# Stick-breaking attention stage rewritten as one unrolled pipeline over four pairs of heads

## The reference

```python
def sb_attend(q, k, v, q_pos0):
    z = jnp.einsum('bqhd,bkhd->bhqk', q, k).astype(jnp.float32) * SCALE
    vis = jnp.arange(nk)[None, :] < (q_pos0 + jnp.arange(nq))[:, None]
    log_fail = jnp.where(vis, jax.nn.log_sigmoid(-z), 0.0)
    log_w = z + lax.cumsum(log_fail, axis=3, reverse=True)
    w = jnp.exp(jnp.where(vis, log_w, NEG))
    out = jnp.einsum('bhqk,bkhd->bqhd', w.astype(v.dtype), v)
```

## Time and profile before

| | us |
|---|---|
| median of 3 runs (1680.41 to 1681.86) | 1681.58 |
| span of the profiled execution, which is also its own time | 1681.6 |
| from the first product of the stage for branch B to its last weighted sum | 409.6 |

### The profile page before, as it was taken

How to read it: one execution, slowest core, us unless ns; L and a number is a source line. 1 busy time by engine, 2 the same in 40 slices (tenths; PEclk the granted TensorE clock), 3 DMA queues, 4 the chain that set the end, 5 groups by cost and what they waited for, 6 DMA issues and landing times.

```text
span 1681.6 us, 27158 instructions
## 1 busy us (share of the span) xinstructions
PE 1590.9 (95%) x9750; PEld 1456.5 (87%) x9750; DVE 767.6 (46%) x1319; ACT 558.3 (33%) x1167; POOL 476.3 (28%) x404
## 2 busy tenths in 40 slices
PE   6998999989898898898999999999999999999996
PEld 5987998878797887897888898998989989899894
DVE  6363473765847668745543313223132231322318
ACT  6354364444443344533333121211212112121123
POOL 2101111342423424242004232322323223232234
PEclk9999999999999999999999999999999999999998
DMA  6111212121021211345222111201112012021123
GB/s 182 49 52 47 61 43 61 44 70 51 25 72 42 57 51 50 122 146 184 105 79 67 50 54 34 62 25 50 57 30 62 27 48 62 26 62 32 43 101 143
DMA packets 129922, 110.44 MB, mean 66 GB/s; under 512 B 14472, under 2 KB 118192, under 8 KB 129872
## 3 DMA queue, kind: packets, MB, share of 16 engines
q1 hardware_dynamic: 122960, 101.11, 19.6%
q10 hardware_dynamic: 6912, 8.65, 1.4%
HBM read 87.94 MB, written 21.80 MB: 65 GB/s over the span
## 4 chain that ended last, share of the span: by engine, by line
PE 77%; issue 9%; DVE 8%; ACT 3%; POOL 1%; DMA 1%; SPq 0%; ACTq 0%; POOLq 0%; DVEq 0%
PE m_ya L1493 20%; PE m_yb L1493 10%; PE m_yb L1515 9%; PE b_gm L893 8%; PE a_gm L443 6%; PE a_gm L479 4%; PE m_ya L1515 4%; DVE b_fail L1073 3%; PE b_gm L915 3%; PE m_ya L1546 3%; PE m_yb L1546 2%; PE b_tb L990 2%; DVE b_wgt L1076 1%; PE a_ob L544 1%; ACT b_wgt L873 1%
## 5 line engine op out<-in xcount | busy, mean ns | idle before, releaser
L1312 POOL TENSOR_TENSOR w_lo<-f_raw,w_hi 128x1024 fp32r<-128x1024 f32 x66 | 157.9, 2399 | 406.5 <-ACT w_hi L1363 406.5
L1493 PE MATMUL m_ya<-x_hi,w_hi 128*128 128x352 f32 x704 | 227.3, 323 | 1.2 <-DVE x_lo L1628 0.9
L1493 PE MATMUL m_ya<-x_lo,w_hi 128*128 128x352 f32 x704 | 225.6, 320 | 0.0
L1493 PE MATMUL m_ya<-x_hi,w_lo 128*128 128x352 f32 x704 | 225.6, 320 | 0.0
L1363 ACT ACTIVATE w_hi<-f_raw 128x1024 fp32r<-128x1024 f32 x66 | 68.2, 1050 | 213.3 <-PE m_yb L1483 209.3
L1493 PEld LDWEIGHTS m_ya<-x_hi,w_hi 128*128 128x128 f32 x704 | 132.0, 188 | 2.5 <-issue 1.0
L1493 PEld LDWEIGHTS m_ya<-x_hi,w_lo 128*128 128x128 f32 x704 | 132.3, 188 | 0.4
L1493 PEld LDWEIGHTS m_ya<-x_lo,w_hi 128*128 128x128 f32 x704 | 132.0, 187 | 0.0
L1681 DVE TENSOR_TENSOR f_yacc<-m_yb,f_yacc 128x512 f32<-128x512 f32 x132 | 90.9, 690 | 82.0 <-PE m_yb L1515 81.6
L1493 PE MATMUL m_yb<-x_hi,w_hi 128*128 128x352 f32 x352 | 113.6, 323 | 0.0
L1493 PE MATMUL m_yb<-x_hi,w_lo 128*128 128x352 f32 x352 | 113.0, 321 | 0.0
(11 more groups left out here) (245 smaller groups left out, 3961.2 us busy)
## 6 DMA issues: line engine op xcount, KB each, us to landing
f_raw<-in_w_gate_up_dram SPq DMA_DIRECT2D x44, 512.0 KB, 3.9
w_raw<-in_w_in_dram SPq DMA_DIRECT2D x33, 512.0 KB, 4.0
f_raw<-in_w_down_dram SPq DMA_DIRECT2D x22, 512.0 KB, 3.4
m_gate<-gate_scratch SPq DMA_DIRECT2D x16, 528.0 KB, 4.3
gate_scratch<-a_gst ACTq DMA_DIRECT2D x24, 176.0 KB, 1.9
gate_scratch<-b_gst ACTq DMA_DIRECT2D x24, 176.0 KB, 1.9
xtok<-in_x_prompt_dram SPq DMA_DIRECT2D x8, 512.0 KB, 3.4
w_raw<-in_w_out_dram SPq DMA_DIRECT2D x8, 512.0 KB, 4.1
```

Source lines behind the costliest of these rows:

```text
L1312: pool.tensor_tensor(w_lo[:, j % 3, :, :].rearrange("p k n -> p (k n)"), raw[:, j % 2, :], w_hi[:, j % 3, :, :].rearrange("p k n -> p (k n ...
L1493: last = pe.matmul(gm[c][:, 0:CW], w[:, j % 3, k, :], x[:, k, chunk(c)], start=(k == 0 and n == 0), stop=(k == KT - 1 and n == 2))
```

## The change

The stage for branch B is no longer a loop: it is written out for all pairs. `ORDER` and `TURN` number all transposes of the stage in one sequence.

- Only q, k and v of the first pair are computed ahead (9 chunks). All other tiles, in the order q, k, v of the next pair and one gate tile, are strewn over the nine steps of the pair before: 288 products in each of the pairs 0 to 2, 348 in pair 3 (five gate tiles), 12 behind it. `STEP` holds the products of each step, and `fills` cuts them into those between the second head's scores, ahead of the transposes, between second groups, and behind the weighted sums.
- `b_qs`, `b_kh`, `b_kl` and `b_vtok` have two buffers, in turn by pair.
- TensorE does transposes and weighted sums of the step before with no products in between, and the rest of the step's products behind the sums. k's and v's tokens of the next pair are turned in steps 6 and 7, the cache's keys in step 5.
- ScalarE: between the first and the second head's sigmoids come the chunks that the first products end (`chunk_out`, with k's and v's copies, which VectorE did) and in step 5 the cache's high parts; behind the output the others. At each tile's second chunk it splits the tile after next.
- GpSimd: both heads' selects, then the low parts of the tiles that are due (`los`).
- VectorE: the first head's scan and multiply, then the cache's low parts, the copies of the turned weights, the tokens, the low parts of chunks (`chunk_out`), then the second head's scan and multiply.
- Outputs of both branches are stored to DRAM (`o_dram`), branch A's by ScalarE's queue at the end of each of its two turns, branch B's in thirds by SP, and loaded for the merge in three chunks. The splits of the first two chunks and of the merge's first weight tile are done within the stage. SP waits for all gate stores ahead of the last chunk.

```diff
@@ branch A, ScalarE
+                    act.wait_ge(o_out, past(g * NSTEP + NSTEP))
+                    act.dma_start(o_dram[bass.ds(g * 2, 2), :, :].rearrange("o p t -> p o t"),
+                                  ot[:, bass.ds(g * 6, 2), :]).then_inc(o_stored, 16)
@@ branch B, the plan
-            FILL = [(0, 3, 0, 3)] * 4 + [(3, 4, 0, 4)] + [(5, 2, 4, 4)] * 3 + [(0, 12, 4, 4), (0, 5, 0, 5)]
+            STEP = [[6, 19, 26, 33, 40, 46, 54, 60, 4]] * (NP - 1) + [[8, 24, 33, 42, 50, 58, 66, 55, 12]]
+            LAST = 12
+
+            def fills(s):
+
+                if s == NS:
+                    return 0, 0, 0, LAST
+                f, i = STEP[s // NT][s % NT], s % NT
+                z, g = f // 8, f // 10 if s and GROUPS[(s - 1) % NT] > 1 else 0
+                rest = f - z * PIECES[i] - 2 * g
+                return z, rest // 2, g, rest - rest // 2
@@ SP, behind the last pair
+                for n in range(2):
+                    sp.wait_ge(gate_stored[n], 16 * KT * NCH // 2)
...
+                for done in (b_out, *b_stored):
+                    sp.wait_ge(*done)
+                load_o(sp, 2)
@@ GpSimd
+                for s in range(NS):
+                    q = ROWS[s % NT]
+                    for a in range(2):
+                        hs = 2 * s + a
+                        pool.wait_ge(z_read, piece(s, a, PIECES[s % NT] - 1) + 1)
+                        for buf, slot, fill in ((fail, hs % NF, 1.0), (wgt, hs % NW, 0.0)):
+                            diag = buf[0:q, slot, SEQ - q:SEQ]
+                            pool.affine_select(out=diag, in_=diag, compare_op=ALU.is_gt, fill=fill, base=0,
+                                               pattern=[[-1, q]], channel_multiplier=1).then_inc(masked, 1)
+                    if s:
+                        los([*chunks(s - 1, False), *chunks(s - 1, True)])
@@ ScalarE
+                    elif kind == 1:
+                        act.activation(kvt[:, chunk(c)], gm[c][:, 0:CW], ACT.Copy).then_inc(vt_ready, 1)
                         for a in range(2):
                             for half in range(2):
+                                last = act.activation(kh[n % 2][half * HD:(half + 1) * HD, a, chunk(c)],
                                                       gm[c][a * HD:(a + 1) * HD, 0:CW], ACT.Copy)
                         last.then_inc(stack_hi, 1)
...
+                    if c == 1 and 3 <= T + 2 < NTILE:
+                        hi(T + 2)
...
+                for s in range(NS + 1):
+                    pair, i = divmod(s, NT)
+                    if s < NS:
+                        for a in range(2):
+                            if a:
+                                for r in chunks(s, False):
+                                    chunk_out(r)
+                                if i == 5:
+                                    for b in range(2):
+                                        act.wait_ge(turned, TURN["c", pair, b] + 1)
+                                        act.activation(kch[:, b, :], tb[TURN["c", pair, b] % 2][:, 0:PAST], ACT.Copy).then_inc(kc_hi, 1)
+                            hs, q, n = 2 * s + a, ROWS[i], KEYS[i]
+                            need(act, w_ready, hs - NF + 1)
...
+                    if s:
+                        out(s - 1)
+                    for r in chunks(s, True):
+                        chunk_out(r)
@@ TensorE
+                        for a in range(2):
+                            for j in range(PIECES[i]):
+                                if a:
+                                    products(at, nz)
+                                    at += nz
+                                z = zb[piece(s, a, j) % 2][0:q, :]
+                                need(pe, z_read, piece(s, a, j) - 1)
...
+                    products(at, na)
+                    at += na
...
+                                t = TURN["w", s - 1, g, a]
+                                if g:
+                                    products(at, ng)
+                                    at += ng
...
+                            pe.wait_ge(turned_out, TURN["w", s - 1, g, 1] + 1)
...
+                    products(at, nc_)
+                    at += nc_
@@ VectorE
+                for s in range(NS + 1):
+                    pair, i = divmod(s, NT)
+                    if s < NS:
+                        weights(s, 0)
+                    if s < NS and i == 5:
+                        for a in range(2):
+                            dve.wait_ge(kc_hi, pair * 2 + a + 1)
...
+                                last = dve.tensor_copy(wt[:, g, a, 0:len(full), 0:q], src[:, 0:len(full), 0:q])
...
+                    if i in (6, 7) and pair < NP - 1:
+                        tok_out("kv"[i - 6], pair + 1)
+                    for r in chunks(s, False):
+                        chunk_out(r)
+                    if s < NS:
+                        weights(s, 1)
+                    for r in chunks(s, True):
+                        chunk_out(r)
```

More of the change, by code:

```diff
@@ L103, in bank, with need @@
         return ctx.enter_context(nc.psum_tensor(name, [P, 512], F32))
+    def need(engine, semaphore, count):
+        if count > 0:
+            engine.wait_ge(semaphore, count)
     with ExitStack() as outer:
@@ L721, in build @@
[L721 to L729 removed]
+            THIRDS = [slice(0, 3 * P), slice(3 * P, 6 * P), slice(6 * P, TOKENS)]
+            BLOCKS = [range(4), range(4, 8), range(8, 9)]
+            W = w_in[0].rearrange("(k p) n -> p k n", p=P)
@@ new lines, in build, with filled @@
+            LAST = 12
[6 more added lines that the diff above has]
+                return z, rest // 2, g, rest - rest // 2
+            def filled(s, end):
+                before = sum(sum(fills(e)[1:]) + fills(e)[2] + fills(e)[0] * PIECES[e % NT] for e in range(s))
+                z, a, g, c = fills(s)
+                return before + (z * PIECES[s % NT] if s < NS else 0) + a + (2 * g + c if end else 0)
@@ L731, in blocks_of, with piece @@
+            TURN = {key: n for n, key in enumerate(ORDER)}
+            def piece(s, a, j):
+                pair, i = divmod(s, NT)
+                return pair * NZ + 2 * sum(PIECES[:i]) + a * PIECES[i] + j
             def blocks_of(i):
@@ new lines, in los @@
+                def los(done):
+                    for r in done:
+                        if r % NCH == 1 and 3 <= r // NCH + 2 < NTILE:
+                            lo(r // NCH + 2)
+                        if r == NCH * (NTILE - 1):
+                            pool.wait_ge(m_first_hi, 1)
+                            pool.tensor_tensor(w_lo[:, 0, :, :], m_raw[0], w_hi[:, 0, :, :].bitcast(F32),
+                                               ALU.subtract).then_inc(m_first_lo, 1)
+                lo(1)
@@ L885, in _ @@
             @block.tensor
             def _(pe):
-                for mine in (gemm_done, turned, z_done, o_done):
-                    pe.sem_inc(mine, CREDIT)
-                def gemm(p, j, c):
-                    for k in range(KT):
-                        for n, (w, x) in enumerate(((w_hi, x_hi), (w_lo, x_hi), (w_hi, x_lo))):
-                            last = pe.matmul(gm[c][:, 0:CW], w[:, SLOT[j], k, :], x[:, k, chunk(c)],
-                                             start=(k == 0 and n == 0), stop=(k == KT - 1 and n == 2))
-                    last.then_inc(gemm_done, 1)
@@ L918, in gates, with tokens @@
                             last.then_inc(gemm_done, 1)
+                def tokens(kind, pair):
+                    for n, blocks in enumerate(BLOCKS):
+                        t = TURN[kind, pair, n]
+                        src = kvt if kind == "k" else vvt
+                        pe.wait_ge(vt_ready, 6 * pair + (3 if kind == "v" else 0) + min(n + 2, NCH))
+                        need(pe, turned_out, t - 1)
+                        for m, i in enumerate(blocks):
+                            last = pe.transpose(tb[t % 2][0:ROWS[i], m * P:(m + 1) * P], src[:, toks(i)], ident[:, :])
+                        last.then_inc(turned, 1)
                 pe.wait_ge(*a_units_split)
```

675 lines of the change are left out of this document (347 added, 328 removed).

## The result

The changed kernel takes 1714.3 us (median of 4 runs, 1710.9 to 1718.2) against 1681.7 (4 runs, 1680.4 to 1683.0): 1.0193 times the time of before, 95% interval 1.0174 to 1.0211, 32.5 us slower. The forecast was 1687, slower, with 1651 to 1704 as its range; the time lies outside.

The account below looks back on a forecast made before the run. TensorE is busy for 95% of the span, so only its waits or slow running can be won. 1681.6 + 0.7 (between branches) + 8.3 (stage) - 3.8 (merge) = 1686.8, say 1687 us, range 1651 to 1704.

Parts of the forecast that it names:

- the term for the clock: Branch B's stage: half clock behind step 5's waits costs 1.4 us in each of three pairs, 4.2 in all.
- Step 5's two waits: Step 5: TensorE waits 2.3 us for ScalarE's reading of scores and 2.2 for the turned cache's copies, together 4.5.
- The waits of 2.4 and 2.3 us: Steps 0 and 8 of a middle pair: TensorE waits 2.4 us in step 0 and 2.3 in step 8.
- Work and waits: Middle pair: 77.7 us of TensorE work and 15.9 of waits.
- The part ahead of the steps: First nine chunks, before the first step: 35.5 us of work, 1.7 of slow clock, 1.0 of waits.
- The first pair's tokens: Pair 0: no wait of step 0 but tokens added, 14.7 us of waits in all.
- The 8.2 us of pair 3 and the 1.5 of the last step: End of the stage: waits of 8.2 us in pair 3, without chunks of q and k, and 1.5 in the last step.
- The seams: Around the stage: 0.7 us more between the branches, 3.8 less before the merge's second tile.
- (a): Stage: pipeline covers most waits, 4.8 us left per pair, time 1647; 1669 if only step 5's go; chance 0.28.
- (b): Stage: waits only change place, losses of 12.7 us per pair as now, time 1679; chance 0.12.
- (c): Steps 3, 5, 7: GpSimd's split locks out scans and TensorE waits, 20 us, time 1707; chance 0.15 for 1698 and above.
- The prediction's last sign: Unrolled code of the stage: a TensorE stall for instructions, shown by no row, would overturn the forecast; no size given.

Follow-up runs that it names:

- e3_merge_splits_moved: Changed kernel with the splits of the merge's input moved out of the last two steps, behind the last pair's step 5 and behind the stage: 1708.0 us.
- e8_copy_for_split: Changed kernel with GpSimd's split of weight tiles in the attention replaced by a plain copy (outputs wrong, for timing only): 1714.4 us.
- e4_idle_filled: Changed kernel with 231 extra, unread products put where TensorE waits in pairs 0 to 2: 1698.4 us.
- e5_scan_last: Changed kernel with VectorE's first scan of a step placed behind the copies of turned weights and of turned tokens: 1700.3 us.
- c2_chunks_before_sums: Changed kernel with products between transposes and sums, another table, scan behind copies in steps 0 and 8, merge splits moved, ScalarE reading chunks before sums: 1657.3 us.
- the four combinations: Four versions of the changed kernel that combine several edits: 1676.5, 1657.3, 1659.2 and 1664.6 us.

## Why the prediction was wrong

**The step that failed** is the term for the clock, in its words "Step 5's two waits, each over 2 us within 6, are like the 2.36 us wait that brought 1.2 GHz: 1.4 us in each of three pairs, 4.2". It gave each pair one fall of the clock, about 3 us at half clock, and only in step 5. The waits of 2.4 and 2.3 us that the same sum has in steps 0 and 8 are as long as the 2.36 us wait of its row, and they were given no fall. The changed kernel's second pair falls in step 5 twice, in step 3, in step 8 and in steps 0 and 1, behind waits of 1.6 to 2.3 us: 20 us at half clock.

What half clock costs can be read from pairs with the same instructions and nearly the same waits. The second pair has 20.5 us at half clock in the changed kernel and takes 102.6 us from its first score to the next pair's; in e3_merge_splits_moved and e8_copy_for_split it has 3.4 and takes 95.2. That is 0.43 us for each us at half clock. The third pair fits, with 13.7 and 99.5. So the 48 us at half clock in pairs 0 to 2 cost some 20.7 us (an estimate from these rows) where the forecast had 4.2: 16.5 of the 26.2 us by which the stage missed. e4_idle_filled is the experiment for it: 16 us in the medians and 17.8 in the traces' stages go with the gaps of these pairs.

**Work and waits** of a middle pair were right. With as much half clock as forecast, a pair takes 95.2 us against 95.0; with none it would take 93.7 against 93.6, so its waits come to 16.0 us against 15.9. Single ones are off: step 1 waits 0.5 us and not 1.1, and step 8 waits 1.6 and not 2.3. The part ahead of the steps took 37.6 us against 38.2. The first pair's tokens are the exception: the sum left 1.2 us for them (14.7 less the 13.5 of a pair without step 0's wait) and they wait 2.83 behind the first scan, as e5_scan_last shows with 0.44. That is 1.6 us.

**A term was missing**: the merge's splits in the last two steps. The 8.2 us of pair 3 and the 1.5 of the last step were those of a pair without them; e3_merge_splits_moved puts them at 5.1 us within the stage. Pair 3 and the last step together are 8.5 us over; the other 3.4 are left to the pair's 10 us at half clock, for which the forecast had nothing, and no experiment separates them. In sum: 16.5 for the clock in three pairs, 1.6 for tokens, 8.5 in the last pair and 0.6 less ahead of the steps make 26.0 of the 26.2 us.

**The seams.** Between the branches the first product starts at 268.66 us, as before at 268.74: 0 and not 0.7. The merge's second tile starts at 731.65, 18.9 us behind the stage against 21.1 before: 2.2 less and not 3.8; its third chunk waits 1.83 for `m_o_lo`, forecast 2.3. 1681.6 + 34.5 - 0.1 - 2.2 = 1713.8 against a span of 1714.9; 1.1 us are not traced.

**The rivals.** (a), that the pipeline covers everything, is wrong for this arrangement, with 13 us or more of waits per pair; c2_chunks_before_sums, at 1657, lies between its two figures, 1647 and 1669, and gets there by other places for products and ScalarE's copies, not by the change as it stands. (b), equal losses, is out. (c) named 1698 and above, and the time is there, but not by its mechanism: in the changed kernel the lock reaches TensorE nowhere, not in step 8 either, where my own sum had put it: with the splits shortened in e8_copy_for_split its waits are the same. In e5_scan_last it is different: a scan of 1024 keys takes 3.81 us beside the split where 2.28 is its own time, and from it VectorE works without a gap up to the weights for which TensorE waits 2.80 us in step 8. No run takes the split away there. The prediction's last sign, a stall for the instructions of the unrolled code, is out as well: every wait of TensorE over 0.4 us in the changed kernel's stage is released by VectorE or ScalarE.

By the Trainium skill, page "SBUF — State Buffer", section "SBUF: two separate sides", the lock holds between a VectorE operation with two SBUF inputs and any GpSimd operation that reads SBUF; the trace of e8_copy_for_split agrees, for a scan of 0.75 us takes 1.55 beside a copy of 1.03. The rule holds here, and it priced nothing: what counted was whether anybody waited for that scan.

Left open is why one wait of 1.5 us brings a fall and the next of 1.9 does not: in the second pair of e3_merge_splits_moved the only fall comes behind a wait of 1.49 us, and those of 1.95, 2.13 and 2.19 bring none. In one execution of e8_copy_for_split the first of two equal pairs has one stretch at half clock and the second six. By the Trainium skill, page "TensorE: Matmul & The Clock Gate", section "Part 1: The HAM clock gate (the "warmup" mystery)", the clock follows recent activity and the moment of a change varies from run to run; the kernels' spread over their runs agrees: 4 to 15 us where such waits stand open, 1 to 3 where most are filled or covered (e4_idle_filled, the four combinations). The time could not have been forecast to the microsecond, but a range could have been: five waits per pair near 2 us, each a fall or none.

## What to carry to other kernels

When an edit opens gaps of one to two microseconds on TensorE, price each gap twice: the idle time, and the products behind it at half clock, which here cost a third as much again (16 to 18 us on some 48 in three pairs); and give the range room for all or none of them to fall. Work that fits anywhere belongs between an operation and the one that waits for its result, not behind both: placed so, the same products were worth 30 us, waits and clock together. When the placement of an instruction is judged, judge it with the cover that it will have: the scan ahead of the copies cost 14 us without products beside it and gained 5 with them.

## What the hardware showed that was not expected

Giving TensorE 231 useless products, 37 us of its time, made the kernel 16 us faster. And two pairs of the same execution, with the same instructions and almost the same waits, took 95.2 and 102.4 us.
